# Routing a mixture of experts in three groups of tiles, with token lists made by products of one-hot matrices

## What is computed

```python
g_logits = h @ w_rg + b_rg                       # 4 groups
g_sel = argmax(g_logits)
g_prob = softmax(g_logits)[g_sel]
e_logits = (h @ w_re + b_re).reshape(n_tok, 4, 8)
top_v, top_i = top_k(e_logits[rows, g_sel], 2)
gate = softmax(top_v) * g_prob
expert = g_sel * 8 + top_i
# each expert's tokens are cut into blocks of 128 rows, in order of token:
y_block = (silu(x @ w_gate[e]) * (x @ w_up[e])) @ w_down[e]
f[token] = sum over its 2 experts of gate * y;  out = LN2(alpha * h + f)
```

## Time and profile before

| | |
|---|---|
| median of 3 runs | 1818.17 us (1817.8 to 1828.08) |
| the profiled execution | 1827.15 us, span 1825.4 us |
| busy PE / PEld / DVE / ACT / POOL | 1634.4 / 1374.9 / 1139.5 / 870.8 / 259.8 us |
| mean granted TensorE clock | 0.943 of full |
| DMA | 315.37 MB, mean 173 GB/s |
| span of the output projection's loop and routing | 827 to 952 us |
| from there to the first expert product | 952 to 1000 us |
| experts | 1000 to 1743 us |
| second LayerNorm and output | 1743 to 1825 us |

### The profile page before, as it was taken

The page is one execution under the profiler, slowest core; times in us unless marked ns, Lnnn a source line. Parts: engine busy times, 40 slices in busy tenths (PEclk is TensorE's granted clock), DMA queues, the critical chain, the costliest instruction groups (busy, mean ns, idle before and its releaser), DMA issues. The chain is left out here.

```text
span 1825.4 us, 27916 instructions
## 1 busy us (share of the span) xinstructions
PE 1634.4 (90%) x9539; PEld 1374.9 (75%) x9540; DVE 1139.5 (62%) x1815; ACT 870.8 (48%) x1354; POOL 259.8 (14%) x282
## 2 busy tenths in 40 slices
PE   8999999988979999978992999999999999999900
PEld 8988888666669999976871778887777887777700
DVE  3466564788752222225888684468886666888856
ACT  3134444666641111113223584467885565878822
POOL 0000000000000000002553111112111111121156
PEclk9999999799889999999995999999999999999955
DMA  4101001600001111114215886769997587999853
GB/s 183 53 24 36 24 24 73 242 1 2 1 36 35 63 40 34 57 56 159 81 50 167 314 330 215 266 251 402 389 406 260 201 332 291 381 401 398 335 173 123
DMA packets 60303, 315.37 MB, mean 173 GB/s; under 512 B 7553, under 2 KB 8337, under 8 KB 35665
## 3 DMA queue, kind: packets, MB, share of 16 engines
q1 hardware_dynamic: 45536, 263.26, 38.0%
q0 software_dynamic: 8944, 30.31, 5.1%
q10 hardware_dynamic: 5760, 20.97, 2.8%
HBM read 271.86 MB, written 42.66 MB: 172 GB/s over the span
## 5 line engine op out<-in xcount | busy, mean ns | idle before, releaser
L1574 DVE TENSOR_TENSOR we_lo<-we_raw,we_hi 128x1024 fp32r<-128x1024 f32 x384 | 449.0, 1218 | 53.7 <-ACT we_hi L1142 53.7
L1142 ACT ACTIVATE we_hi<-we_raw 128x1024 fp32r<-128x1024 f32 x384 | 377.8, 1048 | 71.9 <-issue 42.2
L874 PE MATMUL ps<-we_hi,xb_hi 128*128 128x512 f32 x640 | 257.8, 403 | 5.8 <-DVE we_lo L1574 3.7
L876 PE MATMUL ps<-we_hi,xb_lo 128*128 128x512 f32 x640 | 251.6, 393 | 0.0
L875 PE MATMUL ps<-we_lo,xb_hi 128*128 128x512 f32 x640 | 251.2, 393 | 0.0
L456 PE MATMUL ps<-xT_hi,win_hi 128*128 128x358 f32 (+1 forms) x432 | 145.2, 336 | 8.3 <-DVE win_lo L1234 8.3
L874 PEld LDWEIGHTS ps<-we_hi,xb_hi 128*128 128x128 f32 x640 | 121.1, 189 | 41.1 <-DVE we_lo L1574 13.3
L457 PE MATMUL ps<-xT_lo,win_hi 128*128 128x358 f32 (+1 forms) x432 | 141.3, 327 | 0.0
L876 PEld LDWEIGHTS ps<-we_hi,xb_lo 128*128 128x128 f32 x640 | 121.0, 189 | 26.8
L458 PE MATMUL ps<-xT_hi,win_lo 128*128 128x358 f32 (+1 forms) x432 | 141.0, 326 | 0.0
L875 PEld LDWEIGHTS ps<-we_lo,xb_hi 128*128 128x128 f32 x640 | 121.3, 189 | 23.0
(11 more groups left out here) (308 smaller groups left out, 3217.4 us busy)
## 6 DMA issues: line engine op xcount, KB each, us to landing
we_raw<-w_moe SPq DMA_DIRECT2D x192, 1024.0 KB, 7.9
y_rows<-yb ACTq DMA_DIRECT2D x40, 512.0 KB, 7.9
wmix_raw<-w_mix SPq DMA_DIRECT2D x24, 512.0 KB, 3.4
win_raw<-w_u SPq DMA_DIRECT2D x18, 512.0 KB, 3.4
y_rows<-U SPq DMA_DIRECT2D x1, 8192.0 KB, 33.6
xT_raw<-xT SPq DMA_DIRECT2D x8, 536.0 KB, 8.3
kvb<-U SPq DMA_DIRECT2D x1, 4224.0 KB, 13.3
wout_raw<-w_out SPq DMA_DIRECT2D x8, 512.0 KB, 11.2
```

Of the source, the lines that this page charges most:

```text
L874: pe.matmul(o, xb_hi[:, k, :], e_hi[half][:, c], start=k == 0, stop=False)
L876: last = pe.matmul(o, xb_lo[:, k, :], e_hi[half][:, c], start=False, stop=k == KD - 1)
L1142: act.activation(e_hi[n][:, c], e_raw[n][:, c], ACT.Copy).then_inc(s("e_hi"), 1)
L1574: dve.tensor_tensor(e_lo[n][:, c], e_raw[n][:, c], as_f32(e_hi[n][:, c]), ALU.subtract).then_inc(s("e_split"), 1)
```

## The change

- VectorE only adds the biases for each tile (`take_logits`) and routes three groups at once: `route(0)` for tiles 0 to 3 in the pass of tile 4, `route(1)` for tiles 4 to 6 in the pass of tile 7, `route(2)` for tiles 7 and 8 after the loop. The argmax is made by comparison with the maximum and a falling row of numbers. Each instruction handles a whole group, 22 linked steps to `r_chosen` (23 with a `seen` before it), then two for `exk`.
- TensorE's places come in groups too: `route_places(0)` at k = 4 of tile 5, `route_places(1)` at k = 4 of tile 8, `route_places(2)` after the last logits. The first product counts within each tile, the others add the earlier tiles.
- There is no table in memory, no zeros for it, no indirect writes, no read back. For each tile and each of its two choices, VectorE's `mark` makes a 128x128 one-hot matrix of the slot and a 128x288 matrix with the token's number in the chosen column, and TensorE multiplies and accumulates all 18 in PSUM (`fill_tokens`). Marks 0 to 3 stand behind `norm1(5)`, 4 to 7 behind `norm1(6)`, 8 to 13 behind `norm1(8)`, 14 to 17 after the last place; fills 0 to 3 at k = 3 of tile 6, 4 to 7 at k = 3 of tile 7, 8 to 11 ahead of `turn_rows(8)`, 12 and 13 behind it, 14 to 17 at the end. There are four buffers of each matrix.
- The running sum `cum` is one scan; `tokens` is cast in the middle of the plan.
- The experts' first thirds are rounded and split in the order 2, 0, 1, all ahead of `rest_x(0)`; third 2 has semaphores of its own.
- `ydest` is worked out after the experts' loop; `weights(2)` stands in its place.

```diff
     for t in range(NTL):                       # TensorE, output projection
         for k in range(KD):
             if t == 0:
                 pe.wait_ge(s("o_split"), k + 1)
+            elif k == 3 and t in (6, 7):
+                fill_tokens(4 * (t - 6), 4 * (t - 5))
+            elif k == 4 and t in (5, 8):
+                route_places((t - 5) // 3)
             elif k == 7:
                 turn_rows(t - 1)
...
         if t:
             route_logits(t - 1)
-        if t >= 2:
-            route_places(t - 2)
+    fill_tokens(8, 12)
     turn_rows(NTL - 1)
+    fill_tokens(12, 14)
     route_logits(NTL - 1)
-    route_places(NTL - 2)
-    route_places(NTL - 1)
-    pe.wait_ge(s("r_seen"), NTL)
-    pe.matmul(ps[:, 0, 0:NE], ones, seen[:], start=True, stop=True).then_inc(s("r_count"), 1)
-    pe.wait_ge(s("tokens"), 1)
-    for g in range(3):
-        last = pe.transpose(ps[:, 1, TABR * g:TABR * g + TABR], tab_f[:, g, :], ident[0:TABR, 0:TABR])
+    route_places(2)
+    pe.matmul(ps[:, 0, 0:NE], ones, seen[3][:], start=True, stop=True).then_inc(s("r_count"), 1)
+    fill_tokens(14, 18)
```

```diff
+def route_places(b):                           # TensorE
+    t0, t1 = BATCH[b]
+    o = ps[:, 6, PLACES:PLACES + NE * (t1 - t0)]
+    pe.wait_ge(s("r_chosen"), b + 1)
+    later = [(chosen[:, t, :], t + 1) for t in range(t0, t1 - 1)]
+    if b:
+        later.insert(0, (seen[b], t0))
+    last = pe.matmul(o, sup, chosen[:, t0:t1, :]...)
+    for n, (x, t) in enumerate(later):
+        last = pe.matmul(o[:, NE * (t - t0):]..., ones, x...to_broadcast([P, t1 - t, NE]), ...)
+    last.then_inc(s("r_pos"), 1)
+def fill_tokens(n0, n1):
+    for n in range(n0, n1):
+        M = rows_of(n // 2)
+        pe.wait_ge(s("r_onehot"), n + 1)
+        pe.matmul(ps[:, 7, 0:NCOL], at_slot[n % RING][0:M, :], at_col[n % RING][0:M, :], start=n == 0,
+                  stop=n == 2 * NTL - 1, skip_group_check=True).then_inc(s("r_filled"), 1)
```

```diff
+def first_top(out, m, diff, n, T):             # VectorE; each instruction linked to the next
+    order = falling[:, EPG - n:EPG]...to_broadcast([P, T, n])
+    link(dve.scalar_tensor_tensor(out=m, in0=diff, scalar=0.0, in1=order, op0=ALU.is_equal, op1=ALU.mult))
+    link(dve.tensor_reduce(out, m, AX.X, ALU.max))
+def mark(n0, n1):
+    for n in range(n0, n1):
+        t, k, M = n // 2, n % 2, rows_of(n // 2)
+        if n >= RING:
+            dve.wait_ge(s("r_filled"), n - RING + 1)
+        dve.tensor_tensor(at_slot[n % RING][0:M, :], count[0:M, 0:P],
+                          slot[0:M, t, k:k + 1].to_broadcast([M, P]), ALU.is_equal)
+        dve.scalar_tensor_tensor(out=at_col[n % RING][0:M, :], in0=count[0:M, :],
+                                 scalar=colx[0:M, t, k:k + 1],
+                                 in1=const[0:M, K_TOK + t:K_TOK + t + 1].to_broadcast([M, NCOL]),
+                                 op0=ALU.is_equal, op1=ALU.mult).then_inc(s("r_onehot"), 1)
...
+        if t in (5, 8):                        # VectorE's loop over tiles
+            place((t - 5) // 3)
         norm1(t)
         if t:
-            route(t - 1)
-    route(NTL - 1)
-    place(NTL - 1)
+            take_logits(t - 1)
+        if t in (4, 7):
+            route((t - 4) // 3)
+        if t in (5, 8):
+            mark(*((0, 4) if t == 5 else (8, 14)))
+            weights((t - 5) // 3)
+        if t == 6:
+            mark(4, 8)
+    take_logits(NTL - 1)
+    route(2)
+    place(2)
+    mark(14, 18)
...
+    rest_third(2, 0)
     rest_third(0, 0)
     rest_third(1, 0)
     rest_x(0)
-    rest_third(2, 0)
```

More of the change, by code:

```diff
@@ L256, in build @@
         assert r.at <= work
-        tab_i = r.take("tab_i", [TABR, 3, P], I32)
-        tab_f = r.take("tab_f", [TABR, 3, P])
-        tokens = r.take("tokens", [P, NE * NTL], I32)
+        tokens = r.take("tokens", [P, NCOL], I32)
+        at_col = [r.take(f"at_col{n}", [P, NCOL]) for n in range(RING)]
+        count = r.take("count", [P, NCOL])
+        seen = [r.take(f"seen{n}", [P, NE]) for n in range(len(BATCH) + 1)]
         assert r.at <= work
@@ L800, in route_logits @@
                     pe.wait_ge(s("r_read"), t)
+                done = sum(t >= t1 for _, t1 in BATCH)
+                if done:
+                    pe.wait_ge(s("r_loc"), done)
                 for k in range(KD):
@@ L1187, in more_blocks @@
                         round_h(1, more)
-            for n in range(3):
+            for n in (2, 0, 1):
                 round_third(n, 0)
+            route_exp(2)
             act.preload_act_table_set(SILU_SET)
@@ L1430, in _ @@
             dve.wait_ge(s("m_out"), 3 * KD + 1)
-            link(dve.memset(rt[:], -3e38))
-            link(dve.memset(seen[:], 0.0))
-            link(dve.memset(onehot[:], 0.0))
+            link(dve.memset(lg[:], 0.0))
             def ms_rest(t):
@@ L1501, in place @@
[L1501 to L1513 removed]
+                dve.tensor_tensor(lg[0:M, t, :], ps[0:M, 6, 0:NR], rbias[0:M, :], ALU.add).then_inc(s("r_read"), 1)
@@ new lines, in weights @@
+            def weights(b):
+                t0, t1 = BATCH[b]
+                t = slice(t0, t1)
+                dve.wait_ge(s("r_exp"), 2 * b + 2)
+                link(dve.tensor_reduce(gsum[:, t, :], gexp[:, t, :], AX.X, ALU.add))
+                link(dve.scalar_tensor_tensor(out=eden[:, t, :], in0=second[:, t, :], scalar=1.0, in1=gsum[:, t, :],
+                                              op0=ALU.add, op1=ALU.mult))
+                link(dve.reciprocal(prow[:, t, 0:1], eden[:, t, :]))
+                link(dve.tensor_tensor(prow[:, t, 1:2], prow[:, t, 0:1], second[:, t, :], ALU.mult))
@@ L1536, in _ @@
             link(dve.tensor_scalar(nblk[:], nblk[:], 1.0, None, ALU.max))
-            link(dve.tensor_copy(cum[0][:], nblk[:]))
-            a, d = 0, 1
-            while d < NE:
-                link(dve.tensor_tensor(cum[1 - a][:, d:], cum[a][:, d:], cum[a][:, :NE - d], ALU.add))
-                link(dve.tensor_copy(cum[1 - a][:, :d], cum[a][:, :d]))
-                a, d = 1 - a, 2 * d
-            total = cum[a]
+            total = cum[0]
+            link(dve.tensor_tensor_scan(total[:], ones[:, 0:NE], nblk[:], 0.0, ALU.mult, ALU.add))
+            dve.wait_ge(s("r_filled"), 2 * NTL)
+            dve.tensor_copy(tokens[:], ps[:, 7, 0:NCOL]).then_inc(s("tokens"), 1)
             dve.tensor_scalar(last_blk[:], total[0:1, :], -1.0, None, ALU.add).then_inc(s("plan"), 1)
@@ L1629, in _ @@
             rest_h(1, 0)
+            weights(2)
+            more_blocks(0, 0)
+            with dve.Fori(1, NE) as e:
+                b = dve.value_load(last_blk[0:1, bass.ds(e - 1, 1)], min_val=0, max_val=MAXBLK - 2) + 1
+                new_expert(b, e)
+                more_blocks(e, b)
             link(dve.tensor_tensor(first_row[:], total[:], nblk[:], ALU.subtract))
@@ L1637, in _ @@
             link(dve.tensor_reduce(yfirst[:], own, AX.X, ALU.add))
-            for t in range(NTL):
-                M = rows_of(t)
-                link(dve.tensor_tensor(ydest[0:M, t, :], yfirst[0:M, 2 * t:2 * t + 2], loc[0:M, t, :], ALU.add))
-            dve.tensor_copy(ydest_done[:], total[:, 0:1]).then_inc(s("ydest"), 1)
-            more_blocks(0, 0)
-            with dve.Fori(1, NE) as e:
-                b = dve.value_load(last_blk[0:1, bass.ds(e - 1, 1)], min_val=0, max_val=MAXBLK - 2) + 1
-                new_expert(b, e)
-                more_blocks(e, b)
+            dve.tensor_tensor(ydest[:].rearrange("p t k -> p (t k)"), yfirst[:], loc[:].rearrange("p t k -> p (t k)"),
+                              ALU.add).then_inc(s("ydest"), 1)
             def shift2(t):
```

230 lines of the change are left out of this document (121 added, 109 removed).

## The result

The changed kernel takes 1838.38 us (median of 4 runs, 1837.25 to 1851.41); the kernel before, now with 4 runs, 1821.04 us. The ratio is 1.0105, 95% interval 1.0071 to 1.0139: slower by 13 to 25 us, beside 21.6 forecast. The profiled execution took 1837.25 us with a span of 1835.3 us.

What follows compares the result with a forecast made beforehand. TensorE, nearly always busy outside the tail, was taken as the bound. Loop +22.1, tail +4.2 and behind block 0 -4.7 gave +21.6 us on the median of 1818.17: 1839.8, say 1839 us, range 1832 to 1846.

Steps and rivals of the forecast that it cites:

- The waits: TensorE at k = 4 of tiles 5 and 8 stands 6.2 us each for r_chosen, held by GpSimd's gain and shift: +12.4 us.
- places and clock: In the output projection loop: two grouped places of four products each, +1.8 us; lower clock after each long TensorE wait, +3.6.
- rival B: Short instructions of VectorE and GpSimd don't hold each other, TensorE waits 1.5 us twice: +4.5 us, 1823 us; chance 0.15.
- Marks caught in tiles 6 and 7: The last of four marks waits for GpSimd's gain, so TensorE waits at its fills: +1.6 us twice, +3.2.
- The fills: Eight fp32 products over 288 columns on TensorE in tiles 6 and 7, 0.48 us each: +3.8 us.
- Places removed: Six of the seven old per-tile places on TensorE, 0.45 us each, no longer stand ahead of norm1(8): -2.7 us.
- The loop: Output projection with LayerNorm and routing, up to norm1(8): places, fills, waits, clock and marks together +22.1 us.
- The tail: From norm1(8) to the first expert product: 2.1 + 4.6 - 1.6 - 0.9 = +4.2 us.
- Behind block 0: After the experts' first block, ydest leaves VectorE's queue, expert 1's split comes earlier, TensorE's gap shrinks to 0.6 us: -4.7 us.
- C: Rival: not slower; grouped steps finish before the gain begins, TensorE never stands at k = 4: -1.8 us, 1816 us; chance 0.07.
- D: Rival: more is caught (two marks, one more route step, longer dips): +7 to +9 us more, 1848 us; chance 0.13.

## Why the prediction was right, and where its terms were not

**The waits (+12.4 forecast, +10.9 measured; with places and clock +17.8 against +17.3).** The mechanism held step by step, in both tiles: TensorE at k = 4, two held steps, one to the end of the gain and one to the end of the shift, r_chosen at N + 13.0 in the fifth step (13.3 forecast) and N + 12.4 in the eighth, the half clock behind it (1.8 forecast; 1.8 and 2.6 measured). Taking away the two GpSimd instructions takes 11.4 us from F, which rules rival B out: short instructions are held like long ones. The Trainium skill, "SBUF — State Buffer", section "Who interferes with whom", says that a VectorE instruction with two SBUF inputs contends with a GpSimd instruction that reads SBUF, and that the one that issues second waits for the whole of the first. The trace agrees for these steps of 24 and 32 elements: 2.31, 2.16, 2.04 and 2.00 us.

**Marks caught in tiles 6 and 7 (+3.2 forecast, 0 measured).** This step failed. The four marks took 2.6 us where 2.5 were estimated, and rstd took no time from them (0.63 us beside them, 0.55 in a tile without marks): the last at_col began 0.2 us before the gain, where the sum had the gain first. What stood behind the marks was caught instead, in tile 5 two steps of weights(0) (2.13 and 2.23 us) and in tile 6 ms_lo (2.53 us), and had slack. The fills were +3.7 (3.8 forecast). Places removed: -2.2 (2.7). The loop: -2.2 + 17.3 + 3.7 = +18.8.

**The tail (+4.2 forecast, +8.9 measured).** To the end of the last logits the tail is 5.25 us longer, where 2.1 was forecast: the sum had the marks meet gain and shift, and missed that rstd is held by six of them in a row, +3.6; the fills between are the other 1.6. The run with four marks moved ahead shows it, 4.21 against 1.69 us. That rstd is held here and not in tiles 5 and 6 is in no row of before, and no run shows what decides it. From there to the plan 11.4 us (11.3 forecast). The plan took as long as before (11.5 us), where 1.6 less was forecast: VectorE stood 1.77 us for the last fills at half clock; as fp32r that wait is gone. From the plan to the first product -1.1 (-0.9), ended by VectorE's splits, as the moved third shows.

**Behind block 0 (-4.7 forecast, -7.7 measured).** Moving ydest alone in the kernel before gives -4.4 there: this term was right. The other 3.3 us, 1.9 in the experts' blocks and 1.5 behind the last product, didn't come with ydest. They are in each variant of the changed kernel (the last part 86.1 to 86.4 us in all of them, 87.7 in both forms of the kernel before). The traces show where they lie. The last store of y lands 1.94 to 1.96 us after its issue in every kernel; the span ends 3.5 us behind that in both forms of the kernel before, and 1.9 behind it in all the others. GpSimd's closing DRAIN ends last there, 8.83 us long before and 7.27 after:

```profile
L137 POOLq DRAIN  x1: 8830/8830/8830, 1816.3 to 1816.3; - x1
```

```profile
L139 POOLq DRAIN  x1: 7271/7271/7271, 1827.8 to 1827.8; - x1
```

So the 1.5 us aren't in LayerNorm 2. Of the 1.9, 0.4 is in the second block and the rest 0.05 to 0.1 in many others. Which part of the change does either (GpSimd's 18 table writes are gone, for one) wasn't tested and stays open.

So the total was close partly because errors cancelled: -3.3 in the loop, +4.7 in the tail, -3.0 behind it. C fell with the wait of 5.78 us, and D with the marks that weren't caught.

What the change removed was cheap: places and the table's way were hidden or 0.35 us a tile. What it added was small too, but was put where TensorE reaches it 6 us ahead of its operand. In the last kernel, with the places where TensorE meets them ready, the marks in idle time, the third expert split behind x and fp32r fills, the same algorithm is 28 us of F better than the change as made, and 8 better than the kernel before, of which ydest's move, by its size there, is about half.

## What to carry to other kernels

When work for TensorE is grouped, compute when its operand is ready, held steps included, and put the product where the queue reaches it after that; then ask the same of whatever prepares the next operand, since the move only passes the wait on. When a run of two-input VectorE instructions is added, look at which tiny GpSimd instruction starts beside it, and whether something hangs on that one. Take each edit's cover from the kernel it will stand in: the marks that were free with a late TensorE cost their full time once it was on time.

## What the runs showed of the hardware beyond that

- A short GpSimd instruction that starts beside a run of unlinked two-input VectorE instructions was held to the end of the whole run in some places and not in others. Held: rstd of tile 8 (32x1), 0.57 us beside no marks, 1.69 beside two and 4.21 beside six; and a 1x1 instruction in the tail of the changed kernel, 12.32 us beside the expert splits (1004.03). Not held: rstd of tiles 5 and 6 (128x1), 0.63 and 0.62 us beside four marks; and in the kernel before, beside the same kind of splits, two instructions that took 1.04 and 1.05 us (988.43 and 989.55), each until one split had ended. What decides wasn't found. Behind linked steps the two engines took turns.
- A product of 288 columns takes 0.48 us as f32, in two instructions, and 0.13 as fp32r, in one, at full clock and by their starts. The seventh step, with four of them, fell by 1.37 us.
- After waits of 5.78 and 5.16 us of TensorE the granted clock was 0.50, 0.61 and 1.00, and 0.50, 0.50 and 0.68, in the three windows of 2 us behind them. The price of a long wait differs by up to 1.5 us from one place to the next; the fifth step was 22.34 us in one kernel and 23.8 in two others that were edited elsewhere, with the same wait in all three.
